# Attention logits in three rounded passes, with x in DRAM during the mixing stage, in a two-layer hybrid trunk

## The reference, cut to what matters

```
q = rope(rms_norm(q), positions);  k = rope(rms_norm(k), positions)
score = indexer scores, causal;  keep the 128 best keys of each query
logits = einsum("bqhd,bqkhd->bhqk", q, k_selected) / 8
prob = softmax(logits where valid);  out = prob @ v_selected
...
x = x + merged @ w_out          # the only use of x after the norm of the mixing stage
```

## Time and profile before

| what | value |
|---|---|
| median of three runs | 2742.84 us (2742.21 to 2742.92) |
| profiled execution: its time | 2742.97 us |
| profiled execution: its span | 2741.2 us |
| instructions | 42858 |
| busy: TensorE, VectorE, ScalarE, GpSimd | 2735.9, 1927.5, 1374.6, 970.2 us |
| DMA | 285.19 MB, mean 104 GB/s |

### The profile page before, as it was taken

One profiled execution on the slowest core, in us unless ns is written; L12 is line 12 of the kernel. 1 busy time (PEld: TensorE's weight loads), 2 busy tenths in 40 slices (PEclk: granted clock), 3 DMA queues, 4 the chain that ended last, 5 costly groups with the idle time before them and its releaser, 6 DMA issues.

```text
span 2741.2 us, 42858 instructions
## 1 busy us (share of the span) xinstructions
PE 2735.9 (100%) x16342; PEld 2344.8 (86%) x16342; DVE 1927.5 (70%) x3192; ACT 1374.6 (50%) x2215; POOL 970.2 (35%) x482
## 2 busy tenths in 40 slices
PE   9999999999999999999999999999999999999999
PEld 8898888777788889999998988887777888899998
DVE  7686857885667447888785778578856674588885
ACT  6353444655355446455563534446553653454553
POOL 0134824433343442232121357244333434432331
PEclk9999999999999999999999999999999999999999
DMA  5333583222222223233332335732222222323322
GB/s 171 108 107 117 150 181 109 78 76 70 85 85 85 85 93 101 93 116 105 108 108 93 116 115 156 175 108 78 77 70 80 90 81 89 97 93 104 108 102 100
DMA packets 113262, 285.19 MB, mean 104 GB/s; under 512 B 35632, under 2 KB 45360, under 8 KB 112560
## 3 DMA queue, kind: packets, MB, share of 16 engines
q1 hardware_dynamic: 113072, 282.61, 33.2%
HBM read 268.93 MB, written 9.44 MB: 102 GB/s over the span
## 4 chain that ended last, share of the span: by engine, by line
PE 99%; DVE 0%; DMA 0%; ACT 0%; issue 0%; SPq 0%; ACTq 0%; DVEq 0%
PE bank L653 21%; PE bank L654 21%; PE bank L655 21%; PE bank L702 8%; PE bank L703 8%; PE bank L704 8%; PE bank L679 1%; PE bank L680 1%; PE bank L681 1%; PE bank L1117 1%; PE bank L1136 1%; PE bank L1151 1%; PE bank L886 1%; PE bank L1250 1%; PE bank L1104 0%; PE bank L1309 0%
## 5 line engine op out<-in xcount | busy, mean ns | idle before, releaser
L495 POOL TENSOR_TENSOR w_lo<-raw,w_hi 128x1024 fp32r<-128x1024 f32 x208 | 519.9, 2503 | 872.1 <-ACT w_hi L487 872.1
L653 PE MATMUL bank<-h_hi,w_hi 128*128 128x512 f32 x1504 | 593.3, 395 | 0.5 <-DVE silu_a L2502 0.3
L655 PE MATMUL bank<-h_hi,w_lo 128*128 128x512 f32 x1504 | 585.9, 390 | 0.0
L654 PE MATMUL bank<-h_lo,w_hi 128*128 128x512 f32 x1504 | 585.8, 390 | 0.0
L567 POOL TENSOR_TENSOR w_lo<-raw,w_hi 128x1024 fp32r<-128x1024 f32 (+1 forms) x138 | 253.0, 1854 | 765.7 <-DVE bank L2423 695.3
L487 ACT ACTIVATE w_hi<-raw 128x1024 fp32r<-128x1024 f32 x294 | 309.3, 1056 | 287.6 <-PE bank L655 249.6
L653 PEld LDWEIGHTS bank<-h_hi,w_hi 128*128 128x128 f32 x1504 | 282.3, 188 | 65.7 <-issue 7.1
L655 PEld LDWEIGHTS bank<-h_hi,w_lo 128*128 128x128 f32 x1504 | 282.3, 188 | 59.9
L654 PEld LDWEIGHTS bank<-h_lo,w_hi 128*128 128x128 f32 x1504 | 282.5, 188 | 56.4
L1692 ACT ACTIVATE t_hi<-bank 128x512 fp32r<-128x512 f32 x276 | 162.6, 599 | 207.1 <-DVE bank L2421 61.7
L653 PE MATMUL bank<-g_hi,w_hi 128*128 128x512 f32 x570 | 222.1, 390 | 0.0
(11 more groups left out here) (494 smaller groups left out, 6226.0 us busy)
## 6 DMA issues: line engine op xcount, KB each, us to landing
raw<-in_w_lots SPq DMA_DIRECT2D x478, 512.0 KB, 3.6
s_wd<-s_z SPq DMA_DIRECT2D x8, 512.0 KB, 2.7
s_t<-s_taps SPq DMA_DIRECT2D x16, 256.0 KB, 11.0
da_s<-da_qk SPq DMA_DIRECT2D x16, 256.0 KB, 4.1
x<-in_x SPq DMA_DIRECT2D x8, 256.0 KB, 5.5
raw_k<-in_w_lots SPq DMA_DIRECT2D x8, 256.0 KB, 5.8
s_w_im<-s_wd SPq DMA_DIRECT2D x32, 64.0 KB, 4.2
s_w_re<-s_wd SPq DMA_DIRECT2D x32, 64.0 KB, 3.0
```

Of the source, the lines that this page charges most:

```text
L495: eng.tensor_tensor(w_lo[:, s], raw[:, s], w_hi[:, s].bitcast(f32), SUB).then_inc(S["lo_done"], 1)
L653: pe.matmul(b[:, :], w_hi[:, s, kw], xh[:, k], start=(k == 0), stop=False)
L654: pe.matmul(b[:, :], w_hi[:, s, kw], xl[:, k], start=False, stop=False)
L655: return pe.matmul(b[:, :], w_lo[:, s, kw], xh[:, k], start=False, stop=(k == nk - 1))
```

## The change

- The logits of units 4 to 15 (b of 1, 2 and 3) are made from rounded parts of q and k: high x high, high x low, low x high, accumulated in PSUM, with both heads in turn in each pass. Units 0 to 3 are as before.
- In `att(0)` to `att(3)` ScalarE, after its exponentials, makes the high parts of the head pair's q tile and k tile, and VectorE, after the masking, their low parts; these go where `da_qk` was, so they wait for the unit's own logits too.
- The high parts need eight tiles. They stand in x's place: SP writes x out to DRAM (8 x 256 KB) between the loads of lots 87 to 91, ScalarE waits for that before the first high part, and SP loads x again with lots 152 to 159, once the last logits are made. `out(0)` waits for it.
- Three semaphores get longer names (`da_rot_done`, `da_rms`, `c_pos`), since they now count for more than one thing.

```diff
+        da_qk_hi = at("da_qk_hi", [P, 8, SEQ], f32r, X_AT)
+        da_qk_lo = at("da_qk_lo", [P, 8, SEQ], f32r, A + 13)
...
                 hp, b = UNITS[u]
                 if u > 1:
                     pe.wait_ge(S["da_max"], 2 * u)
+                if b:
+
+                    pe.wait_ge(S["da_rot_lo_done"], 8 + 2 * (hp + 1))
+                    w = P * (b + 1)
+                    for first, (q_part, k_part) in enumerate(((da_qk_hi, da_qk_hi), (da_qk_hi, da_qk_lo), (da_qk_lo, da_qk_hi))):
+                        for e in range(2):
+                            r = slice(64 * e, 64 * e + 64)
+                            m = pe.matmul(logit_bank(u, e)[:, 0:w], q_part[r, hp, P * b:P * (b + 1)], k_part[r, 4 + hp, 0:w],
+                                          start=first == 0, stop=first == 2, skip_group_check=True)
+                    m.then_inc(S["da_logit"], 1)
+                    return
...
+                def spill_x(first, to):
+                    sp.wait_ge(S["h_done"], H(3 * KT))
+                    for i in range(first, to):
+                        sp.dma_start(X_SPILL[i], x[:, i]).then_inc(S["c_pos_x_moved"], 16)
+
                 for n in (-1, 0, 1):
                     lot_after(next_lot + n)
+                    spill_x(n + 1, n + 2)
                 sp.wait_ge(S["da_rope"], 4)
                 halves_across(1)
-                for n in (2, 3):
-                    lot_after(next_lot + n)
-                ring(MIX0 // 4 + 6, turn)
+                lot_after(next_lot + 2)
+                spill_x(3, 5)
+                lot_after(next_lot + 3)
+                spill_x(5, 8)
+                ring(MIX0 // 4 + 6, turn - 7)
+                sp.wait_ge(S["da_logit"], PAIRS)
+                sp.wait_ge(S["c_pos_x_moved"], x_out_at())
+                for i in range(KT):
+                    lot_after(4 * (turn - 7) + i)
+                    sp.dma_start(x[:, i], X_SPILL[i]).then_inc(S["c_pos_x_moved"], 16)
+                ring(turn - 5, turn)
...
@@ ScalarE, the end of att(u)
+                if b == 0:
+
+                    act.wait_ge(S["c_pos_x_moved"], x_out_at())
+                    act.wait_ge(S["da_rot_lo_done"], 8)
+                    for j in (hp, 4 + hp):
+                        act.activation(da_qk_hi[:, j], da_qk[:, j], AFT.Copy).then_inc(S["da_rms_hi"], 1)
...
@@ VectorE, out(i)
+                if i == 0:
+                    V.wait_ge(S["c_pos_x_moved"], x_back_at())
...
@@ VectorE, the end of att(u)
+                if b == 0:
+
+                    V.wait_ge(S["da_logit"], u + 1)
+                    for e, j in enumerate((hp, 4 + hp)):
+                        V.wait_ge(S["da_rms_hi"], 8 + 2 * hp + e + 1)
+                        TT(da_qk_lo[:, j], da_qk[:, j], da_qk_hi[:, j].bitcast(f32), SUB).then_inc(S["da_rot_lo_done"], 1)
```

More of the change, by code:

```diff
@@ L412, in trunk @@
             gel_hi_done gel_done glu_y_done y_hi_done y_done small_psum small_done merge_used da_sq da_low da_ms
-            da_ln da_rms da_shifted da_rope da_rot_done da_rel da_relu da_score da_logit da_max da_exp da_rec da_prob
+            da_ln da_rms_hi da_shifted da_rope da_rot_lo_done da_rel da_relu da_score da_logit da_max da_exp da_rec da_prob
             da_pt_psum da_pt_ready da_pv da_o_done m2_dtb m2_abs m2_dt_ready m2_acs m2_acs_sum m2_acs_hi m2_acs_lo m2_sel m2_acs_turn
@@ L417, in trunk @@
             hg_op hg_o hg_ex hg_sq hg_rms hg_yn hg_lc hg_el""".split()
-        ONCE = """act_seq dve_seq pool_seq mix_clear c_ones_g_lo c_rest c_pos x0_in_t_hi x1_in_prod x2_in_piece x3_in_xcopy x4_in_g_sum x5_in_yv x6_in_g_hi x7_in_t_sum w0_in_t_lo
+        ONCE = """act_seq dve_seq pool_seq mix_clear c_ones_g_lo c_rest c_pos_x_moved x0_in_t_hi x1_in_prod x2_in_piece x3_in_xcopy x4_in_g_sum x5_in_yv x6_in_g_hi x7_in_t_sum w0_in_t_lo
             p_hi p_lo p_step p_ang p_trig p_seq e_out""".split()
@@ L543, in gs_at, with x_out_at, x_back_at @@
             return 4 * site_at(which, th) + i + 1
+        X_SPILL = nc.dram_tensor("x_kept", (KT, P, SEQ), f32, kind="Internal").ap()
+        def x_out_at():
+            return 48 + 16 * KT * (2 * OUT.layer + 1)
+        def x_back_at():
+            return 48 + 16 * KT * (2 * OUT.layer + 2)
         def raw_ready(eng, n):
@@ L1155, in att_start @@
             def att_start():
-                pe.wait_ge(S["da_rot_done"], 8)
+                pe.wait_ge(S["da_rot_lo_done"], 8)
                 logits(0)
@@ L1388, in _ @@
             sp.dma_start(con[:, 0:upper], con_in[:, 0:upper]).then_inc(S["c_ones_g_lo"], 16)
-            sp.dma_start(pos_i[:, :], positions.partition_broadcast(P)).then_inc(S["c_pos"], 16)
-            sp.dma_start(con[:, freq:NCON], con_in[:, freq:NCON]).then_inc(S["c_pos"], 16)
-            sp.dma_start(gam[:, :, :], gamma_in).then_inc(S["c_pos"], 16)
+            sp.dma_start(pos_i[:, :], positions.partition_broadcast(P)).then_inc(S["c_pos_x_moved"], 16)
+            sp.dma_start(con[:, freq:NCON], con_in[:, freq:NCON]).then_inc(S["c_pos_x_moved"], 16)
+            sp.dma_start(gam[:, :, :], gamma_in).then_inc(S["c_pos_x_moved"], 16)
             for layer in range(DEPTH):
@@ L2009, in gate @@
                 else:
-                    act.wait_ge(S["da_rot_done"], 8)
+                    act.wait_ge(S["da_rot_lo_done"], 8)
                 act.activation(gate_th[:, i % 2], bank[t % 4][:, :], AFT.Tanh, scale=0.5).then_inc(S["free%d" % (t % 4)], 1)
@@ L2109, in da_norm @@
                     act.wait_ge(S["da_ln"], 4 * g + j + 1)
-                    act.activation(da_t[g][:, j], da_t[g][:, j], AFT.Exp, scale=-0.5).then_inc(S["da_rms"], 1)
+                    act.activation(da_t[g][:, j], da_t[g][:, j], AFT.Exp, scale=-0.5).then_inc(S["da_rms_hi"], 1)
             def da_index(b):
@@ L3015, in da_norm @@
                 for j in range(4):
-                    V.wait_ge(S["da_rms"], 4 * g + j + 1)
+                    V.wait_ge(S["da_rms_hi"], 4 * g + j + 1)
                     V.wait_ge(S["da_rope"], 4 * g + j + 1)
-                    TT(da_qk[:, 4 * g + j], da_qk[:, 4 * g + j], da_t[g][:, j], MUL).then_inc(S["da_rot_done"], 1)
+                    TT(da_qk[:, 4 * g + j], da_qk[:, 4 * g + j], da_t[g][:, j], MUL).then_inc(S["da_rot_lo_done"], 1)
             def da_index(b):
@@ L3309, in pdo @@
                     p.need(p.do(ins))
-                V.wait_ge(S["c_pos"], 48)
+                V.wait_ge(S["c_pos_x_moved"], 48)
                 pdo(V.tensor_copy(ang[:, 2], pos_i[:, :]))
```

1 line of the change is left out of this document (removed).

## The result

| what | before | after |
|---|---|---|
| median | 2742.66 us (2742.21 to 2742.92, four runs) | 2761.4 us (2760.41 to 2762.73, four runs) |
| ratio | | 1.0069 (1.0056 to 1.0081) |
| span of the profiled execution | 2741.2 us | 2758.6 us |
| from the first transposes of att(0) to those of att(15), layer 0 and 1 | 124.03, 124.03 us | 133.96, 132.50 us |

The change makes the kernel 0.69% slower. 2754.2 us was forecast with 2747.5 to 2761.0 as the range, so the sign and the place are as forecast, and the size is 0.4 us beyond the end of the range. The last line of the table holds nearly all of the difference: 9.93 + 8.47 = 18.4 of the 18.7 us between the medians. Layer 0 of the changed kernel begins it 0.81 us earlier (533.85 instead of 534.66 us), so a time of before stands here for one 0.81 us smaller.

The account below looks back on a forecast made before the run. TensorE, busy 2735.9 of 2741.2 us, was taken as the bound. Per layer +6.5 us of stalls less 0.8 gained is +5.7, two layers +11.4, giving 2754.2 us, 0.42% slower; range 2747.5 to 2761.

Parts of the forecast that it names:

- The mechanism: VectorE's in-order wait for ScalarE's high parts stalls TensorE in att(3) to att(7): chance 0.70, 2748.5 to 2760 us.
- The walk: Step-by-step lateness of VectorE, ScalarE and TensorE from att(0) on: each layer loses about 6.5 us.
- the 9.6 forecast: By att(7), VectorE 9.6 us late against TensorE's 6.0, so 3.6 us between them.
- The lock: At att(0), VectorE's two-SBUF-input subtractions starting inside GpSimd's weight split are held until it ends: about 0.45 us.
- the step at att(0): Low parts end at about 541.15 after GpSimd's split ends at 539.92; VectorE is 4.2 us late.
- The gain: Shorter logits on TensorE, limited by ScalarE's copy before the second transpose: 0.8 us a layer in the last six steps.
- The wait is not short: Rival: high parts ready before VectorE has masked unit u+2, no stall of note, 2740.5 to 2741.5 us; 0.14 including a halfway case.
- the heads overlap: Rival claimed the opposite: rounded passes of both heads run in series, 1.7 us a layer lost, 2759 us; chance 0.07.
- the full cut does not arrive: Rival claimed it does: neither copy nor VectorE matters in the logits, 6.0 us less, 2737 us; chance 0.02.
- TensorE's clock does fall: Rival: after attention stalls TensorE runs at 1.2 GHz, six us of it per layer giving 2760 us; chance 0.07.
- about 2 us of the queue for a write: Each write of x takes about 2 us of SP's queue, costing TensorE nothing unless the queue is several lots behind.

Follow-up runs that it names:

- low_on_pool: Changed kernel with GpSimd making the low parts behind its own weight split, instead of VectorE: 2742.21 us, beside 2742.70 before the change.
- change_no_lock: Changed kernel with GpSimd splitting only 8 of 1024 columns of each mixing-stage weight lot (values wrong): 2753.81 us, beside 2742.52 before the change.
- logits_no_lock: logits_only with GpSimd splitting only 8 of 1024 columns of each mixing-stage weight lot: 2740.5 us, beside 2742.52 before the change.
- wait_only: Changed kernel where VectorE waits for the high parts but makes no low parts; passes read other ones (values wrong): 2753.9 us, beside 2742.62 before.
- logits_only: Changed kernel whose three passes read rounded data already there, so no high or low parts are made (values wrong): 2742.21 us, beside 2742.70 before.
- one_pass: logits_only with the high x high pass alone instead of three passes (values wrong): 2741.63 us, beside 2742.70 before the change.
- filler: Changed kernel with the logit passes of units 4 to 6 made four times over, results the same: 2763.72 us, beside 2742.62 before the change.
- no_wait: Changed kernel where ScalarE and VectorE make parts from data long ready, so VectorE does not wait (values wrong): 2750.48 us, beside 2742.62 before.
- high_early: Changed kernel where ScalarE makes all eight high parts in one go before att(0): 2752.42 us, beside 2742.62 before the change.
- x_only: Only x's trip to DRAM and back kept; logits as before, no high or low parts: 2742.69 us, beside 2742.70 before the change.

## Why the prediction was too low

**The mechanism: as forecast, shown.** low_on_pool takes VectorE's wait and its work away, and the loss goes with them; in the kernels without long splits the wait alone makes 13.1 us (2753.81 and 2740.67).

**The walk: right up to the holds.** Moved by 0.81 us, it has the low parts of att(0) done at 540.34 (measured: 538.59 + 1.67 = 540.26). The reciprocals of att(1) to att(4) were forecast for 544.6, 553.2, 563.6 and 572.5 and stand at 546.12, 554.61, 565.10 and 574.02. Every one is 1.4 to 1.5 us later than forecast, from the first on, and between 540.26 and 546.12 the only instruction that is longer than before is the comparison, by 1.98 - 0.29 = 1.69 us. The second hold adds 2.29 - 0.36 = 1.93 us. Then VectorE is 13.07 us late at 599.07 (586.81 before) instead of the 9.6 forecast: 3.5 more, and the two holds are 3.6. TensorE's first transposes of att(9) follow, 10.0 us late instead of 6.5. In layer 1 the first comparison is held again and the second not (1.97 and 0.36 us), and the loss is 1.5 us smaller:

```profile
1918.02 1.97 DVE L3089 TENSOR_SCALAR da_mb<-da_mb 128x256 f32<-128x256 f32 x1
...
1954.11 0.36 DVE L3089 TENSOR_SCALAR da_mb<-da_mb 128x384 f32<-128x384 f32 x1
```

**The step that failed.** The lock was a term of the walk, sized at 0.45 us a layer, 0.9 in all: the step at att(0) asked only whether the new subtractions start inside a split. It did not ask it of VectorE's other instructions, all of which are moved against GpSimd's splits by being late, and it took only operations with two SBUF inputs for holdable. Measured, the holds cost 7.6 us over both layers. That is 6.7 us more than forecast, and the time is 7.2 us above the forecast's 2754.2. Without holds the walk gives 6.2 us a layer, and a time of about 2753.5 us was expected for change_no_lock; it has 6.45 and 6.15 from att(0) to att(9), and 2753.81 us. That this agrees to tenths is in part luck, since up to 0.8 and 0.6 us of it are the clock's (below), which the walk put at nothing.

**The gain: right in size, lost in the change.** Forecast at 0.8 us a layer for the last six steps, it is 0.84 from att(8) to att(14) in logits_no_lock, and 0.98 in the whole stretch. In the changed kernel it does not arrive: layer 0 is 9.95 us late at att(9), 9.4 at att(13), and after the held convolution before att(14) 9.93 at att(15). In layer 1 it is 8.52 at att(9) and 8.47 at att(15). So the sum's term of -0.8 a layer was nothing, by a hold again.

**The rivals.** The wait is not short (wait_only), the heads overlap (logits_only), and the full cut does not arrive (one_pass). TensorE's clock does fall, which I had given 0.07. After the stalls of att(4) the changed kernel's windows show (us; busy of TensorE, weight loads, VectorE, ScalarE, GpSimd; granted clock; DMA share; GB/s):

```profile
568.64:575.96 7.32, 7.32 (x27) 5.91 (x27) 6.94 (x24) 3.56 (x9) 2.38 (x1) 0.77 0.17 49
1942.55:1950.64 8.09, 8.09 (x26) 6.49 (x27) 7.68 (x25) 4.20 (x10) 2.38 (x1) 0.68 0.19 67
```

The same 27 matmuls took 5.73 us before (563.01 to 568.74). The granted 0.77 and 0.68 are means over stretches partly at 1.2 and partly at 2.4 GHz. What did that cost? As the kernels fall into it in some layers only, they can be compared. In wait_only the fall comes in layer 0 alone:

```profile
565.51:573.91 8.40, 8.40 (x27) 6.69 (x27) 7.95 (x26) 4.20 (x10) 2.37 (x1) 0.66 0.19 62
1934.71:1940.44 5.73, 5.73 (x27) 4.70 (x27) 5.42 (x18) 2.51 (x5) 2.40 (x1) 1.00 0.01 3
```

Layer 0 is 2.67 us longer here, and over the whole stretch 0.6 us shorter than layer 1 (129.24 and 129.82). That does not show that the fall was free, because layer 1 has the held comparison instead. To price the fall, look at how long the scaled probabilities had been ready when TensorE took them at att(7) and att(8), after it. If they were ready long before, TensorE was late by itself, and the slow matmuls count; if they came just then, VectorE set the time, and the matmuls only filled it. In wait_only, layer 0, they were ready 1.98 and 1.73 us before; up to 1.7 us there are the clock's by this estimate. In the changed kernel, before att(7) of layer 0 (its transpose at 592.30) and before att(8) of layer 1:

```profile
591.74 0.91 ACT L2171 ACTIVATE da_p<-da_p,da_st 128x256 f32<-128x256 f32 x2 [4.08 <-DVE da_st L3107]
...
1971.24 1.13 ACT L2171 ACTIVATE da_p<-da_p,da_st 128x384 f32<-128x384 f32 x2 [1.96 <-DVE da_st L3107]
1972.74 0.49 PE L1157 MATMUL bank<-con,da_p 128*128 128x128 f32 x3
```

In layer 0 the first head's probabilities were ready 0.05 us before the transpose of att(7), so nothing is the clock's there. In layer 1 the least is 0.88 us, before att(8), so by the same estimate at most 0.9 of the 18.7 us is the direct cost of slow matmuls. In change_no_lock it is at most 0.84 and 0.57 us. The changed kernel's first fall, 3.41 us from 558.4, cost nothing: it is in layer 0 alone, and both layers come to att(4) 32.01 us after their first transposes. So the rival's 2760 us is near the measured time, and so are its six us of half clock a layer (6.8 measured), but its mechanism is not what made the time.

The clock has a second effect. In both layers of the changed kernel the second comparison starts 46.35 us after the first transposes. The split starts at 46.03 in layer 0 and holds it; in layer 1, where TensorE had 6.83 us at half clock before it, at 46.35, and it is then the split that is lengthened:

```profile
1954.11 2.62 POOL L497 TENSOR_TENSOR w_lo<-raw,w_hi 128x1024 fp32r<-128x1024 f32 x1 [6.58 <-ACT w_hi L489]
```

In the change, wait_only, filler, no_wait and high_early there are ten such layers. In eight the split starts 0.32 or 0.33 us before the comparison and holds it. In the two with 6.83 us at half clock between att(4) and att(5) it starts with the comparison or 0.84 us behind it, and nothing is held. (The Trainium skill, "TensorE: Matmul & The Clock Gate", part 1, has idle time throttle the array. The trace agrees that it fell behind stalls, in layer 0 of the change of 1.31 us before the first fall and of 0.55 and 1.42 us with work between them before the second. But no_wait and high_early have stalls of up to 1.4 and 1.5 us and no fall.)

**What stays open.** That the splits hold these comparisons rests on the start times, on the layers in which the split came later and on the kernels in which all splits are short; no kernel moved a single split. That the fall of the clock is what moved the split in those two layers is the likely reading and was not tried. The exact cost of the clock stays open too, within the bounds above: no kernel here has these stalls in both layers at the full clock.

## What to carry to other kernels

When a step makes an in-order engine late, its own waits and its own work are only two of three terms. The third is that all it does afterwards lands elsewhere against the other engines, and where two of them exclude each other, as some operations of VectorE and GpSimd do here, an operation of that kind that falls into the other's is lengthened, here by up to 2.2 us of the other's 2.4. So before sizing such an edit, list the other engine's long operations and slide the late engine's list along them, all of its operations and not only the new ones; and if work must be added, put it on the engine whose operations do the holding and behind them in its order, as low_on_pool does: it cost nothing there and 18.7 us on VectorE.

A bound can stand in no wait at all: the second transposes began 0.15 us after ScalarE's copy and showed no idle time until one_pass took the logits away.

## What the runs showed of the hardware

- A comparison of 128x256 or 128x384 f32 with one SBUF input is held by a GpSimd subtraction as those with two are: 1.98 instead of 0.29 us, 2.29 instead of 0.36. The top-k's MAX8 and MATCH_REPLACE8 are not: inside the split from 560.80 to 563.19 of the changed kernel they take 0.56 and 0.54 us, as elsewhere.
- The hold goes both ways. Where VectorE's pair started 0.01 us before the split (550.54 and 550.55), the split took 2.93 us instead of 2.40 and the pair 3.49 instead of 1.28: the first subtraction delayed the split, and the split the second.
- Rounded passes on two groups of 64 rows start at most 0.01 us apart, as plain f32 ones do, and three of them over 512 columns took 0.17 us less than the plain product (0.89 and 1.06), not a quarter of it.
- At the lower clock the passes of a weight lot, 512 columns, started 0.427 us apart instead of 0.227 (558.6 to 561.6 in the changed kernel). The granted clock fell behind stalls of 0.5 to 2.2 us each, with TensorE busy between them; in no_wait, with stalls of up to 1.4 us, it did not fall.
- SP's writes of x (256 KB) took 5.1 us from issue to landing and the loads back 3.8 us (medians), and neither cost time (x_only); the forecast had about 2 us of the queue for a write.
